# RWKV-7 recurrence on one core: the products with K on the array's other two 64x64 tiles

## The reference, cut to what matters

```python
def step(S, inp):
    r_t, w_t, k_t, v_t, kk_t, a_t = inp
    sa = jnp.einsum("bhvk,bhk->bhv", S, -kk_t)
    S = (S * w_t[:, :, None, :] + sa[..., None] * (kk_t * a_t)[:, :, None, :]
         + v_t[..., None] * k_t[:, :, None, :])
    o_t = jnp.einsum("bhvk,bhk->bhv", S, r_t)
    return S, o_t
```

## Time and profile before

| what | value |
|---|---|
| median of 3 runs | 1936.94 us (1934.85 to 1938.9) |
| the profiled execution | 1946.07 us, span 1944.0 us |
| granted clock, mean | 0.978 |
| busy in the span: PE, DVE, ACT, POOL | 93%, 54%, 41%, 13% |
| the recurrence | about 497 to 825 us of the span |
| slots with an AB | 16 |

### The profile page before, as it was taken

One profiled execution on the slowest core, in us unless ns is written; L12 is line 12 of the kernel. 1 busy time (PEld: TensorE's weight loads), 2 busy tenths in 40 slices (PEclk: granted clock), 3 DMA queues, 4 the chain that ended last, 5 costly groups with the idle time before them and its releaser, 6 DMA issues.

```text
span 1944.0 us, 43902 instructions
## 1 busy us (share of the span) xinstructions
PE 1813.3 (93%) x18432; PEld 1544.3 (79%) x18432; DVE 1051.4 (54%) x1718; ACT 798.9 (41%) x1459; POOL 250.2 (13%) x315
## 2 busy tenths in 40 slices
PE   7999999999899999999999998999999998777797
PEld 6988999999888888799986776777776775343697
DVE  6744363553489999445445444443463444677334
ACT  4234233233466677433333323333334444555233
POOL 0300000000255555232000000000000000110032
PEclk9999999999999999999999999999999999898899
DMA  7534554555345553244889999999999999999541
GB/s 277 198 132 165 178 179 154 169 177 174 90 124 141 144 137 95 89 152 150 333 308 417 390 410 417 416 425 426 425 425 399 416 426 350 419 378 362 216 148 73
DMA packets 154200, 510.45 MB, mean 263 GB/s; under 512 B 60097, under 2 KB 81986, under 8 KB 108738
## 3 DMA queue, kind: packets, MB, share of 16 engines
q1 hardware_dynamic: 153442, 503.66, 68.7%
q10 hardware_dynamic: 576, 4.19, 0.6%
HBM read 472.86 MB, written 32.32 MB: 260 GB/s over the span
## 4 chain that ended last, share of the span: by engine, by line
PE 32%; DMA 18%; DVE 3%; issue 2%; ACT 2%; SPq 1%; DVEq 0%; ACTq 0%
DMA at_vraw<-in_cache_v 18%; PE psP L2626 8%; PE psP L2627 7%; PE psP L2628 7%; PE at_psO L2680 5%; PE at_psS L2659 3%; SPq L2039 1%; PE psP L2725 0%; DVE wlo L2388 0%; PE at_psT L2671 0%; DVE at_o_new L2543 0%; DVE at_p_rc L2571 0%; DVE at_w L2476 0%; ACT at_p_w L2346 0%; ACT at_p_w L2344 0%
## 5 line engine op out<-in xcount | busy, mean ns | idle before, releaser
L2626 PE MATMUL psP<-xhi,whi 128*128 128x320 f32 x1488 | 476.7, 320 | 3.0 <-DVE xlo L2513 2.0
L2627 PE MATMUL psP<-xlo,whi 128*128 128x320 f32 x1488 | 461.5, 310 | 0.0
L2628 PE MATMUL psP<-xhi,wlo 128*128 128x320 f32 x1488 | 461.4, 310 | 0.0
L2626 PEld LDWEIGHTS psP<-xhi,whi 128*128 128x128 f32 x1488 | 281.3, 189 | 67.0 <-issue 65.5
L2388 DVE TENSOR_TENSOR wlo<-wraw,whi 128x2048 fp32r<-128x2048 f32 x92 | 212.9, 2314 | 210.5 <-ACT whi L2214 210.2
L2214 ACT ACTIVATE whi<-wraw 128x2048 fp32r<-128x2048 f32 x92 | 176.1, 1914 | 279.5 <-PE psP L2628 278.2
L2627 PEld LDWEIGHTS psP<-xlo,whi 128*128 128x128 f32 x1488 | 281.7, 189 | 0.1
L2628 PEld LDWEIGHTS psP<-xhi,wlo 128*128 128x128 f32 x1488 | 281.2, 189 | 0.0
L139 PE MATMUL psP<-xhi,whi 128*128 128x320 f32 x704 | 218.1, 310 | 2.6 <-DVE wlo L174 2.3
L140 PE MATMUL psP<-xlo,whi 128*128 128x320 f32 x704 | 217.5, 309 | 0.0
L141 PE MATMUL psP<-xhi,wlo 128*128 128x320 f32 x704 | 217.5, 309 | 0.0
(11 more groups left out here) (374 smaller groups left out, 3078.5 us busy)
## 6 DMA issues: line engine op xcount, KB each, us to landing
wraw<-in_weights SPq DMA_DIRECT2D x156, 1024.0 KB, 6.0
at_kraw<-in_cache_k SPq DMA_DIRECT2D x96, 1024.0 KB, 11.0
at_vraw<-in_cache_v SPq DMA_DIRECT2D x94, 1024.0 KB, 10.9
at_kraw<-in_cache_k SPq DMA_DIRECT2D x64, 512.0 KB, 9.4
at_vraw<-in_cache_v SPq DMA_DIRECT2D x62, 512.0 KB, 10.1
rw_s0t<-in_s0T SPq DMA_DIRECT2D x16, 256.0 KB, 3.6
o_wkv_s<-rw_SN SPq DMA_DIRECT2D x16, 256.0 KB, 2.9
wraw<-in_weights ACTq DMA_DIRECT2D x4, 1024.0 KB, 6.3
```

What stands on the lines that cost most here:

```text
L2626: pe.matmul(out, wh, c_.xhi[:, kc, :], start=(kc == 0), stop=False)
L2627: pe.matmul(out, wh, c_.xlo[:, kc, :], start=False, stop=False)
L2628: last = pe.matmul(out, wl, c_.xhi[:, kc, :], start=False, stop=(kc == NM - 1))
```

## The change

Three things. First, AB's products with Kz are written to the other head's partitions of their bank: Kz of head 0 gives its result on partitions 64 to 127 and that of head 1 on 0 to 63. So for each chunk the four matmuls lie on the four 64x64 tiles of the array. Second, the mask step KK, one operation of 128 partitions by 512, becomes two of 64 partitions by 512, each of which reads the other head's partitions and writes its own. Third, `ORDER` is new throughout (the same 121 steps), and waits are set anew to fit it: SP's load of k waits for sq and kk0 too, bonus waits for oy of three tiles before, W waits for A12 in each tile, ST1 for SP1, O3 for SA3, SA0 for XB, and SA4 and var join the steps whose bank is waited for.

```diff
-P.t.s4 F.a.sq P.t.Ht R.g.Vnx F.a.kk0 P.t.AB P.v.s3 P.a.Ht P.v.Bt P.v.D4s F.v.cs R.t.mean F.a.Pi F.g.csm P.v.D F.a.ka1
-R.t.U0 P.t.XB R.v.cen F.g.k2 R.t.Q4 P.v.Dt P.a.XB R.a.U0 P.v.KK P.a.Bn P.g.ID R.t.SA0 P.t.D2 R.a.Q4 R.v.SA0 R.a.csq
-P.v.FR R.t.S0 P.a.D2 R.t.U4 R.v.ST0 R.t.var P.a.A12 P.v.D2t R.a.U4 R.a.SP1 R.t.U1 P.v.Vn R.a.lnv R.t.SA4 P.t.W F.v.rk
-R.a.U1 R.a.SA4 F.a.Pc R.t.SA1 P.t.D4t R.a.rstd R.v.SA1 F.g.Rz P.v.W F.t.ss R.v.on P.a.D4t F.a.Pm R.t.S1 P.t.Y R.a.ong
-R.v.ST1 F.v.ssm R.t.U2 R.g.oy P.v.Y R.t.O1 F.a.ln F.t.bon R.a.U2 P.v.Yt R.a.SP2 R.g.SAx R.a.O1 F.a.rn R.t.SA2 P.t.E
-R.v.SA2 P.v.Kt R.t.S2 P.a.E R.t.SN R.v.ST2 P.a.Kn P.v.Et R.a.SP3 F.v.kk P.t.Z1 R.v.SNa F.g.ka R.t.U3 P.v.Z1 P.t.E2t
-R.a.U3 F.g.Kz F.v.Az R.t.O2 P.a.E2t R.t.SA3 R.t.O0 R.a.O2 R.g.y R.v.SA3 P.t.X F.v.Bz R.a.O0 R.t.O4 P.v.X R.g.SNb
-R.t.S3 R.a.O4 R.t.O3 P.v.X1t R.a.xh F.v.bonus R.a.O3 R.v.xl R.v.ST3
+R.g.Vnx R.t.mean R.t.U0 R.a.U0 P.t.Ht R.v.cen P.t.s4 P.a.Ht F.v.cs R.a.csq P.t.XB P.t.AB P.v.Bt P.a.XB F.a.Pc P.v.s3
+F.a.Pi P.v.D4s R.t.SA0 R.t.Q4 P.v.D F.a.ka1 R.v.SA0 P.a.Bn P.v.Dt F.g.k2 R.t.S0 P.v.FR R.a.Q4 P.t.D2 F.a.sq F.g.csm
+R.v.ST0 R.t.U4 P.v.KK R.t.U1 R.a.U4 F.t.ss R.a.U1 F.g.Rz R.a.SP1 P.a.D2 R.t.SA1 R.t.SA4 R.t.var P.a.A12 R.v.SA1
+P.v.D2t F.a.kk0 P.g.ID R.t.S1 F.v.ssm R.a.SA4 R.a.lnv P.t.D4t R.v.ST1 F.g.Kz F.v.rk P.t.W P.a.D4t R.g.SAx R.t.U2 P.v.W
+R.t.O0 R.a.U2 R.t.O1 R.a.rstd P.v.Vn R.t.SA2 P.t.Y R.a.O0 R.a.O1 R.v.SA2 F.a.Pm R.v.on R.t.S2 R.a.SP2 P.v.Y R.a.ong
+R.t.SN F.a.ln P.v.Yt R.g.oy R.v.ST2 F.a.rn P.t.E R.v.SNa R.a.SP3 R.g.y R.t.U3 P.a.E P.v.Kt F.t.bon R.a.U3 P.v.Et
+R.t.O2 F.v.kk R.t.SA3 P.t.Z1 R.a.O2 R.v.SA3 P.a.Kn F.g.ka F.v.Az P.t.E2t P.v.Z1 R.t.O4 R.g.SNb P.a.E2t F.v.bonus
+R.t.O3 R.a.xh P.t.X F.v.Bz R.a.O3 R.a.O4 R.t.S3 P.v.X P.v.X1t R.v.xl R.v.ST3
...
+                F.a.wait(sp, F.a.last("sq", "kk0"), t)
                 F.g.wait(sp, "k2", t)
                 load("k", t + 1)
...
-                        Q.v.done(dve.tensor_tensor(pair(KK[t % 2][:]), pair(quads[:, ak]),
-                                                   flat(c_.mSI[:]).unsqueeze(1).to_broadcast([P, NCH, 2 * L]), ALU.mult), name)
+                        for h in range(2):
+                            here, there = slice(L * h, L * h + L), slice(L * (1 - h), L * (1 - h) + L)
+                            masked = dve.tensor_tensor(pair(KK[t % 2][here]), pair(quads[there, ak]),
+                                                       flat(c_.mSI[there]).unsqueeze(1).to_broadcast([L, NCH, 2 * L]), ALU.mult)
+                        Q.v.done(masked, name)
...
-                            for out, lhs in ((ps, zt[0]), (other, zt[1])):
-                                for r in halves:
-                                    last = pe.matmul(out[r, cc], lhs[r, c], flat(ar[r, c]),
+                            for out, lhs, swap in ((ps, zt[0], 0), (other, zt[1], 1)):
+                                for h, r in enumerate(halves):
+                                    last = pe.matmul(out[halves[h ^ swap], cc], lhs[r, c], flat(ar[r, c]),
                                                      start=True, stop=True)
...
-                        if t == 0:
-                            Q.a.wait(pe, "A12", t)
+                        Q.a.wait(pe, "A12", t)
```

More of the change, by code:

```diff
@@ L434, in products_of_chunk @@
     return pe.matmul(out, wl, c_.xhi[:, kc, :], start=False, stop=(kc == NM - 1))
-STILL_READ = {"s4": "v.D4s", "X": "v.X", "S3": "v.ST3", "mean": "v.cen", "O0": "a.O0", "O1": "a.O1", "SN": "v.SNa"}
+STILL_READ = {"s4": "v.D4s", "X": "v.X", "S3": "v.ST3", "mean": "v.cen", "SA4": "a.SA4", "var": "a.lnv", "O0": "a.O0", "O1": "a.O1", "SN": "v.SNa"}
 class Banks:
@@ L1200, in front @@
                         F.a.wait(pool, "ka1", t)
+                        loaded(pool, "k", t)
                         F.g.done(pool.tensor_tensor(k2[:], k2[:], ins["k"][:], ALU.mult), name)
@@ L1253, in front @@
                     if name == "Pc":
+                        F.v.wait(act, "cs", t)
                         if t >= 3:
@@ L1408, in front @@
                         loaded(dve, "v", t)
+                        if t >= 3:
+                            R.g.wait(dve, "oy", t - 3)
                         F.v.done(dve.tensor_tensor(BONUS[t % 3][:], psF[:, 0:TOK], ins["v"][:], ALU.mult), name)
@@ L1503, in run @@
                         else:
-                            if c == 2:
-                                R.a.wait(dve, "SP2", t)
+                            if c < 3:
+                                R.a.wait(dve, f"SP{c}", t)
                             R.v.done(dve.scalar_tensor_tensor(out=ST[c][:], in0=ps, scalar=last_of_chunk(t, c),
@@ L1727, in run @@
                             R.a.wait(pe, f"U{c}", t)
+                            if c == 0:
+                                Q.a.wait(pe, "XB", t)
                             R.t.done(both(ps, [(X[j][:, c], U[:])]), name)
@@ L1734, in run @@
                         else:
-                            if c < 2:
+                            if c != 2:
                                 R.v.wait(pe, f"SA{c}", t)
```

## The result

The changed kernel takes **1950.92 us** (median of 5 runs, 1946.18 to 1955.2) against 1936.94 for the kernel before in the same comparison (5 runs, 1934.47 to 1938.9): ratio 1.0067, 95% interval 1.0049 to 1.0085. It is slower by 0.7%; the forecast was 1931.5, and the range ended at 1942. The profiled execution took 1955.2 us, its span 1953.5, 9.5 us more than the span of 1944.0 before.

The account below looks back on a forecast made before the run. It took one loop through nearly full TensorE and VectorE to bound each slot. 15 intervals x 0.29 = 4.4, plus 1 in the first slot, saved 5.4 us: 1931.5 us from 1936.94, range 1923 to 1942.

Parts of the forecast that it names:

- The short AB: AB's 32 records on TensorE, on four overlapping tiles, go from 1.78 to 0.93 us: minus 0.85.
- rival D: The four tiles don't overlap, AB stays 1.78 us, the loop is 16.91: 1943.4 us; chance 0.06.
- The mask: K's mask on VectorE, split into two operations of 64 partitions by 512, costs 0.58 us extra a slot.
- The base: The slot shown in the recurrence, 16.35 us from AB to AB, against which the new loop was set.
- AB to D: Leg of the slot's loop from AB's first product to step D: 2.12 us before, 1.16 after.
- The walk of the new order: Hand sum of the slot's legs in the new order, by one slot's durations: 16.06 us, saving 0.29 a slot.
- D to W: Leg of the slot's loop from step D to W, with both masks: 4.85 us before, 5.11 after.
- Z1 to X1t: Leg of the slot's loop from Z1 through bonus, Bz and X: 2.91 us before, 2.01 after.
- Waits the diff adds: SP's later load of k costs nothing unless Bn slips; the other added waits have ended long before.
- Rival C: SP comes late to Kn's moves, Bt waits, each slot is 16.86 us: slower, 1941.6 us; chance 0.15.
- The ends: Outside the repeating slots: about 1 us saved in the first slot with an AB, 0 elsewhere.
- Slots after the last AB: 0: Slots behind the last AB keep their steps, so their time changes by 0.

Follow-up runs that it names:

- e2: The kernel before, in its old order, with AB on four tiles and the mask in two operations: 1952.19 us, ratio 1.0064.
- e8: The kernel before with AB on four tiles and one mask operation, part of the computation changed: 1937.23 us, ratio 0.9999.
- e1: The changed kernel with two buffers for `a`, whose load then stands at the head of the slot: 1946.23 us, ratio 1.0038.
- e9: e5 with each 1 MB weight load cut into four of 256 KB, two in each of slots 3 to 10: 1934.02 us, ratio 0.9973.
- e5: e1 with three pairs of extra, unused matmuls in the first slot after the last AB: 1942.44 us, ratio 1.0013.
- e6: The changed kernel (one buffer for `a`) with three pairs of extra, unused matmuls after the last AB: 1943.14 us, ratio 1.0043.
- e3: The changed kernel, with its new order and waits, but AB on two tiles and one mask operation: 1954.71 us, ratio 1.0081.
- e7: e1 with the mask of K as one operation, part of the computation changed: 1941.91 us, ratio 1.0019.
- e11: The changed kernel with the weight loads cut into 16 of 256 KB and nothing else: 1946.28 us, ratio 1.0043.
- e12: e5 with the 1 MB weight loads kept whole but issued right behind Bn, earlier in the slot: 1935.72 us, ratio 0.9992.

## Why the prediction was wrong, step by step

**The short AB, D against it.** Predicted 0.93 us and four tiles that overlap: measured 1.0. Right, and rival D (no overlap) is out.

**The mask.** Predicted 0.58 extra and two operations of 0.65: measured 2 x 0.688, and 0.70 of slot in the old order (e2 against e8). Right in kind (only the length counts), short by 0.1. The Trainium skill (TensorEngine Tiling (Array Packing), PSUM Bottleneck) says that tiling speeds up TensorE and not the evacuation of PSUM, which may become the bottleneck; in the old order the runs agree: the four tiles alone give nothing (e8, 0.9999), and with the longer evacuation they lose (e2, 1.0064).

**The base.** The sum set 16.06 against the slot shown, 16.35, which was not an undisturbed one: those are 16.22. And the leg "AB to D", 2.12, was counted as part of the path though D waited for nothing at its end, so the AB that it holds could not give anything back there; e8 shows 0.00. The walk of the new order came to 16.06, measured 16.18 (of its legs, D to W was 5.50 in the middle slot instead of 5.11, where rk took 1.25 us beside GpSimd). That the walk came within 0.12 is in part luck: this leg is 0.4 longer, and Z1 to X1t is 0.27 shorter (1.74 instead of 2.01), since Bz took 0.61. Gain per undisturbed slot 0.04, not 0.29: 3.8 us of the forecast's 5.4 gone, and the forecast would have been "no change". Two smaller slips: the leg AB to D adds up to 1.14 and not 1.16, and the gain was counted from the one slot of 16.35, the losses of C and D from the average of 16.48.

**The step that made it slower: "Waits the diff adds".** The text said that the waits in SP's queue cost "nothing unless Bn slips", and named the load of k, s, r, v and g. It left out the load of `a`, which stands behind Kn's moves in SP's queue and moved with them, 1.3 us later in the slot, while its reader ka1, ahead of Bn, came 0.5 us earlier against D. That closes a loop through SP: Kn's moves, `a`, ka1, Bn, Bn's moves, the loads, Kn's moves. Its slack, 1.2 us by the medians, was used up, so that a delay is passed on: 10.1 us of waits at ka1 in 200 us, and 17.01 us for the average slot without a weight load, where two buffers for `a` (e1) give 16.27. The clue stood in the rows: Kn's moves at 652.73 in the slot shown are 10.6 after D, where the median of before is 9.7, so the one slot that was walked made the new place look hardly later. Rival C had the queue as its mechanism and a slower kernel as its result, but its price a slot, 16.86, was below the 17.17 measured, and its place, Bt behind Kn's moves, holds only a part (4.0 us; over 0.3 us in four slots, not in most). e1, which takes the loop away, takes back 0.3% of 0.67% by the medians.

**A moved step's DMAs.** The weight loads go with the place of Vn and moved 2.4 us later into the slot. The prediction didn't count them. Cutting and spreading them is worth 0.4% by the medians (e9 against e5, whose intervals are apart).

**The ends.** "About 1 us saved" in the first slot: D came 2.1 us earlier, but the next interval was 17.99 instead of 15.75 (D waits 2.11 us for AB at 542.92): nothing saved. It goes with the granted clock: from 525 to 540 us this was 0.55 to 0.84 in after, and 1.00 in e5, where the same order had a first interval of 15.25. "Slots after the last AB: 0": TensorE's waits there were followed by the clock at 0.50, and the stretch took 4.6 us more than before (nearly 6 more than in the new order without the fall); the filled kernels e5 and e6 gain about 0.25% by the medians, with overlapping intervals.

**What stays open.** Every D to D interval comes from one profiled execution each, and single executions of one kernel differ by 17 to 21 us (e1, e6). Much of that lies outside the change: from the first scores to the end all fourteen kernels are alike, and this stretch took from 950.4 us (e1's profile) to 962.1 (before's). The split of the 0.67% among the queue, the weight loads and the clock is by medians whose intervals mostly overlap; the waits and the sorted intervals show that the first two lengthen slots, and less surely by how much. Why the clock fell in the profiles of after, e3, e7 and e11 and not in that of e1, whose TensorE idles 1.03 of 4 us at the same place, is not settled. That the 1 MB loads delay TensorE's next instructions or Kn's landing rests on their times and on e9, in which two things changed at once: the size of a load and its place. e12 moved only the place and gave, by the medians, half of it. Which transfer makes Bt wait in e9 wasn't found.

## What to carry to other kernels

In a pipeline whose slot repeats, take as base the shortest interval that recurs, and before a leg is called part of the path look whether the instruction at its end waited at all: one without a wait gives nothing back when its input comes earlier. When an order is rewritten, walk the in-order DMA queue round the whole slot as carefully as the engines, with every load, the ones that keep their place too, up to the reader that stands first in its engine, and note the DMAs that hang on a moved step. When more than one thing can disturb a slot, sort the slots by what happens in each, before medians are compared. A reorder that trades one cost for its equal leaves less slack, and it is the disturbed slots that then decide.

## What the runs showed of the hardware

- 32 records of 128 columns of two pairs on four 64x64 tiles take 1.01 us, 32 ns each, where the sum had 29 from Q4 and Ht; on two tiles they took 1.78, 56 each.
- An operation of 64 partitions by 512 elements from PSUM, which writes the other 64 partitions, takes VectorE 0.688 us, where one of 128 by 512 takes 0.65 to 0.68.
- The load of `a`, 160 KB, lands 2.2 to 4.7 us after its issue in one and the same execution of after (median 3.0).
- 1.04 us of idle time of TensorE in 4 were followed by some 13 us at half clock in the profiled execution of after, and 1.03 in 4 by none in that of e1.
